# Probability copies on two engines, another order of the sample's turns, and identity products behind the norms

## The reference

```
h = rmsnorm(x);  qa,ka,va,qb,kb,vb = h @ w_in          # 8 heads a, 8 heads b (2 kv heads), 64 wide
qa,ka,qb,kb: rmsnorm per head, then rotary on the first 16 columns
oa = dilated attention (windows 128/512/2048, steps 1/4/16, merged by their softmax weights)
ob = attention over the last 128 keys, with a sink per head
x += concat(rmsnorm(oa), rmsnorm(ob)) @ w_out
x += (silu(h2 @ w_gate) * (h2 @ w_up)) @ w_down         # h2 = rmsnorm(x), 2816 hidden columns
```

## Time and profile before

| | us |
|---|---|
| median of three runs (3018.22 to 3023.43) | 3021.51 |
| profiled execution, whole | 3009.97 |
| its span, first to last instruction | 3008.4 |
| attention stage of the first layer | 294 to 600 |
| first layer's FFN | 765 to 1508 |
| second layer | 1511 to 2994 |

### The profile page before, as it was taken

The page is one execution under the profiler, slowest core; times in us unless marked ns, Lnnn a source line. Parts: engine busy times, 40 slices in busy tenths (PEclk is TensorE's granted clock), DMA queues, the critical chain, the costliest instruction groups (busy, mean ns, idle before and its releaser), DMA issues.

```text
span 3008.4 us, 51127 instructions
## 1 busy us (share of the span) xinstructions
PE 2827.9 (94%) x19000; PEld 2607.7 (87%) x19000; DVE 1171.7 (39%) x2420; ACT 916.4 (30%) x1662; POOL 510.6 (17%) x211
## 2 busy tenths in 40 slices
PE   5999999878999999999969999997889999999998
PEld 5999666578999999999969986665889999999998
DVE  5454555443322222222255455554442222322223
ACT  2343665521212111121134346664121111211110
POOL 1221000022112211122022200001222111221110
PEclk7999999978999999999979999998989999999999
DMA  5221544132654454411022144321345544454111
GB/s 162 58 64 56 151 119 111 32 98 98 197 182 158 163 174 155 155 42 55 1 94 61 54 122 128 105 78 40 100 155 166 173 155 155 155 169 155 42 42 58
DMA packets 182636, 333.47 MB, mean 111 GB/s; under 512 B 30352, under 2 KB 142096, under 8 KB 179664
## 3 DMA queue, kind: packets, MB, share of 16 engines
q1 hardware_dynamic: 171632, 195.26, 21.2%
q0 software_dynamic: 2816, 135.99, 13.6%
q10 hardware_dynamic: 8032, 0.17, 0.2%
HBM read 309.15 MB, written 157.94 MB: 155 GB/s over the span
## 4 chain that ended last, share of the span: by engine, by line
PE 89%; DVE 4%; issue 2%; ACT 2%; ACTq 1%; DMA 1%; POOL 0%; SPq 0%; DVEq 0%; POOLq 0%
PE ps L402 69%; PE ps L1422 4%; PE ps L1436 4%; PE ps L1411 3%; PE ps L1335 2%; PE ps L1485 1%; PE ps L1473 1%; DVE g_lo L957 1%; PE ps L1454 1%; DVE t_buf L942 1%; PE ps L1300 1%; DVE hf L952 1%; PE ps L1461 1%; DVE hf L942 1%; ACT pt L762 1%
## 5 line engine op out<-in xcount | busy, mean ns | idle before, releaser
L402 PE MATMUL ps<-g_hi,f_hi 128*128 128x352 f32 x2496 | 812.2, 325 | 36.0 <-DVE g_lo L957 26.9
L402 PE MATMUL ps<-g_hi,f_lo 128*128 128x352 f32 x2496 | 809.4, 324 | 0.0
L402 PE MATMUL ps<-g_lo,f_hi 128*128 128x352 f32 x2496 | 808.3, 324 | 0.0
L402 PEld LDWEIGHTS ps<-g_hi,f_hi 128*128 128x128 f32 x2496 | 473.8, 190 | 38.9 <-DVE g_lo L957 28.7
L623 POOL TENSOR_TENSOR f_lo<-f_raw,f_hi 128x2048 fp32r<-128x2048 f32 x66 | 303.9, 4618 | 1186.3 <-ACT f_hi L874 1186.3
L402 PEld LDWEIGHTS ps<-g_lo,f_hi 128*128 128x128 f32 x2496 | 474.0, 190 | 0.0
L402 PEld LDWEIGHTS ps<-g_hi,f_lo 128*128 128x128 f32 x2496 | 473.9, 190 | 0.0
L1260 DVE TENSOR_TENSOR silu<-silu,ps 128x352 f32<-128x352 f32 x132 | 68.8, 521 | 810.7 <-ACT silu L896 810.7
L1270 DVE TENSOR_TENSOR xm<-xm,ps 128x352 f32<-128x352 f32 x528 | 271.2, 521 | 199.4 <-PE ps L402 199.4
L402 PE MATMUL ps<-a_hi,f_hi 128*128 128x352 f32 x1056 | 340.6, 323 | 0.0
L402 PE MATMUL ps<-a_hi,f_lo 128*128 128x352 f32 x1056 | 338.4, 320 | 0.0
(11 more groups left out here) (167 smaller groups left out, 3473.4 us busy)
## 6 DMA issues: line engine op xcount, KB each, us to landing
out_dram<-in_cache_a_dram POOLq DMA_DIRECT2D x16, 8176.0 KB, 27.2
f_raw<-in_w_gate_up_dram SPq DMA_DIRECT2D x44, 1024.0 KB, 6.4
f_raw<-in_w_down_dram SPq DMA_DIRECT2D x22, 1024.0 KB, 4.9
k_near<-in_cache_a_dram SPq DMA_DIRECT2D x16, 1024.0 KB
v_near<-in_cache_a_dram SPq DMA_DIRECT2D x16, 1024.0 KB
w_raw<-in_w_in_dram SPq DMA_DIRECT2D x28, 512.0 KB, 4.0
k_far<-in_cache_a_dram SPq DMA_DIRECT2D x16, 768.0 KB
v_far<-in_cache_a_dram SPq DMA_DIRECT2D x16, 768.0 KB
```

The source lines that it names most:

```text
L402: mm = pe.matmul(out, left(a, c), right(b, c), start=(start and c == 0 and k == 0), stop=(stop and c == n - 1 and k == 2))
```

## The change

`keep_probs` is split: ScalarE copies the groups of hh = 0, VectorE those of hh = 1, at the end of its step, each with a semaphore of its own, and `turn_probs` and `mix` wait for the owner's. The sample's turns have another order: near 0, far 0, near 1, far 1, near 2 of the next sample (uses 3 to 7), then the first, second and third turn of the probabilities (8 to 10), far 2 (11), `mixed` (12), near 3 (13), the out products (14), far 3 (15). The sinks' exponentials come with the first turn, their sum and inverse with the third, and the spread is four slots. TensorE gets `keep_clock(n, bank)`: n fp32 products of the identity with 512 columns of a mask into a bank that nobody reads: seven ahead of the sums of norms 0 and 1, two ahead of those of norm 3, and at norms 0, 1 and 3 one ahead of the spread and three behind it.

```diff
-        pt_ready = Signal("pt_ready", len(groups))
+        groups_by = [[g for g in range(len(groups)) if groups[g][1] == hh] for hh in range(2)]
+        pt_ready = [Signal(f"pt_ready{hh}", len(groups_by[hh])) for hh in range(2)]
...
         def use_near(b, pr):
-            return 2 * pr if b == 0 else use_of(b - 1, 3 + 2 * pr)
+            return 2 * pr if b == 0 else use_of(b - 1, (3, 5, 7, 13)[pr])
+
+        def use_far(b, pr):
+            return 2 * pr + 1 if b == 0 else use_of(b - 1, (4, 6, 11, 15)[pr])
...
-        TURNS = 9 + 16 * (NB - 1) + 12 + 5 * (NP - 1)
+        TURNS = 9 + 16 * (NB - 1) + 12 + 4 * (NP - 1)
...
-                        sp.wait_ge(s_filled.sem, s_filled.at(l, max(use_near(b - 2, NP - 1) + 1, use_last(b - 2)) + 1))
+                        sp.wait_ge(s_filled.sem, s_filled.at(l, max(use_far(b - 2, NP - 1), use_last(b - 2)) + 1))
...
+                def keep_probs(d):
+                    for g in groups_of[d, 1]:
+                        _, _, a, b = groups[g]
+                        if g >= 4:
+                            dve.wait_ge(mixed.sem, mixed.at(l, groups[g - 4][0] + 1))
+                        dve.wait_ge(p_turned.sem, p_turned.at(l, g + 1))
+                        nc.vector.tensor_copy(pt[:, g % 4, 0:(b - a) * P], ps[:, 0 + g % 2, 0:(b - a) * P]
+                                              ).then_inc(pt_ready[1].sem, 1)
...
                     for _ in range(FILL[2 * (d + 2) + 1]):
                         next(beside)
+                    if 0 <= d < ND:
+                        keep_probs(d)
...
+                        if b in SPREAD_AFTER:
+                            add_sinks(SPREAD_AFTER[b])
+                        yield
+                        if b + 1 < NB:
+                            keep_far(b + 1, 2)
+                            yield
...
+            def keep_clock(n, bank):
+
+                for _ in range(n):
+                    pe.matmul(ps[:, bank, :], ident[:], mask_a[:, 0:512], start=True, stop=True)
+
             def sum_squares(l, k, acc):
 
                 first, n, before, width = NORMS[k]
+                if k in (0, 1):
+                    keep_clock(7, 7)
+                elif k == 3:
+                    keep_clock(2, 7)
                 pe.wait_ge(sq_added.sem, sq_added.at(l, ADDS[k] + n - 1))
...
             def spread_roots(l, k, bank):
 
+                if k != 2:
+                    keep_clock(1, 7)
                 pe.wait_ge(rs_ready.sem, rs_ready.at(l, 2 * k + 2))
...
                 mm.then_inc(rs_spread.sem, 1)
+                if k != 2:
+                    keep_clock(3, 0)
...
                         if g >= 2:
-                            pe.wait_ge(pt_ready.sem, pt_ready.at(l, g - 1))
+                            owner = groups[g - 2][1]
+                            pe.wait_ge(pt_ready[owner].sem, pt_ready[owner].at(l, groups_by[owner].index(g - 2) + 1))
...
-                    pe.wait_ge(pt_ready.sem, pt_ready.at(l, groups_of[d, 1][-1] + 1))
+                    for hh in range(2):
+                        pe.wait_ge(pt_ready[hh].sem, pt_ready[hh].at(l, groups_by[hh].index(groups_of[d, hh][-1]) + 1))
```

More of the change, by code:

```diff
@@ L754, in softmax @@
                                          accum_out=sum_p[:, 2 * d + hh:2 * d + hh + 1]).then_inc(exped.sem, 1)
-                def keep_probs(d, hh):
-                    for g in groups_of[d, hh]:
+                def keep_probs(d):
+                    for g in groups_of[d, 0]:
                         _, _, a, b = groups[g]
@@ L787, in exps_b, with sum_sinks @@
                                          ).then_inc(s_exped.sem, 1)
-                def spread(p):
+                def sum_sinks(p):
                     act.wait_ge(exped.sem, exped.at(l, 32 * p + 32))
@@ L805, in sample @@
                         if b + 1 < NB:
[L806 to L813, removed]
+                            keep_near(b + 1, 0)
+                            exps(b)
+                            yield
+                            exps_b()
+                            yield
+                            keep_near(b + 1, 1)
+                            yield
+                            yield
+                            keep_near(b + 1, 2)
+                            yield
                         else:
@@ L831, in sample @@
                         yield
+                        if b + 1 < NB:
+                            keep_near(b + 1, 3)
+                            yield
                         yield
+                        if b + 1 < NB:
+                            yield
                         if b in SPREAD_AFTER:
[L834 to L839, removed]
+                            for _ in range(4):
+                                yield
                 beside = sample()
@@ L852, in _ @@
                         next(beside)
-                    if 0 <= d < ND:
-                        keep_probs(d, 1)
                 next(beside, None)
-                spread(NP - 1)
+                sum_sinks(NP - 1)
                 meet(act, l, 0)
@@ L1112, in scale_b, with add_sinks @@
                                             ).then_inc(s_sums.sem, 1)
-                def spread(p):
+                def add_sinks(p):
                     dve.wait_ge(sink_exped.sem, sink_exped.at(l, 2 * p + 2))
@@ L1119, in spread @@
                     nc.vector.reciprocal(inv_p[:], sum_p[:, 32 * p:32 * p + 32]).then_inc(sums_ready.sem, 1)
-                    yield
+                def spread(p):
                     dve.wait_ge(mix_kept.sem, mix_kept.at(l, 16 * p + 16))
@@ L1458, in turn_far @@
                 def turn_far(b, pr):
-                    bank = sample_bank(use_near(b, pr) + 1)
+                    bank = sample_bank(use_far(b, pr))
                     for c in range(4):
@@ L1504, in sample @@
                         read(use_near(b, NP - 1))
-                        read(use_near(b, NP - 1) + 1)
                         score_sample(b, 0, 0, WIN)
                         yield
+                        read(use_far(b, NP - 1))
                         score_sample(b, 1, WIN, NKEYS)
@@ L1518, in sample @@
                             keys_in(b + 1)
[L1519 to L1523, removed]
+                            turn_near(b + 1, 0)
+                            yield
+                            turn_far(b + 1, 0)
+                            yield
+                            turn_near(b + 1, 1)
+                            yield
+                            turn_far(b + 1, 1)
+                            yield
+                            turn_near(b + 1, 2)
+                            yield
                         else:
```

47 lines of the change are left out of this document (31 added, 16 removed).

## The result

The changed kernel takes 2998.84 us (median of four, 2998.26 to 2999.71) against 3019.86 for the kernel before (four, 3014.71 to 3023.43) on the same chip: ratio 0.9932, 95% interval 0.9915 to 0.9949. In a later series it was 0.9940 (0.9926 to 0.9954). The forecast was 3001.5. A version in which they fill the waits ahead of the work that follows is faster than both kernels (0.9895).

The account below looks back on a forecast made before the run. TensorE ends nearly every link of the chain of waits, so only shortening or filling its queue helps. Attention 23 us gained less 3 lost at the norms makes 20: 3021.5 to 3001.5, range 2988 to 3020.

Parts of the forecast that it names:

- Wait on the copies: Attention: probability-times-value products wait 18.1 us behind ScalarE's copies; moving hh = 1 to VectorE gains 10 (4 to 18.1).
- The term of VectorE's queue: Attention: copies standing in order ahead of VectorE's masks and drains cost 2.4 us per layer (0 to 22).
- Turn of the probabilities: Attention: the sample's turn no longer stands third behind a bank ScalarE still reads; 4.1 us gained.
- New-order waits: Attention: the sample's new slot order brings waits of its own, 5.1 us lost per layer (0 to 10).
- The three-slot half-steps: Attention: four half-steps per layer hold three slots, the third needing the first's bank; 1.03 us lost each.
- Clock: Attention: half-clock stretches follow stalls that go away; 10 us gained over both layers (0 to 17).
- clock still falls: Rival, 0.18: half-speed stretches of attention stay because thin steps remain; only 10 us gained, 3011.5.
- The rival of VectorE in ScalarE's place: Rival, 0.10: VectorE's in-order copies hold up masks and bank drains, 22 us lost per layer; 3041.
- The 12 us named as the sign of a wrong forecast: Wrong if TensorE's products or scores stand behind VectorE's copies or masks for more than 12 us per layer.
- Norm 1: Three identity products behind the spread stand on the path ahead of norm 2's sums; 1.9 us lost per layer.
- the rival of the later clock: Rival, 0.05: norm 1's spread does not help the clock return, norm 2's sums end 1.9 us later; 3005.
- the products hold the clock: Rival, 0.07: identity products keep full clock at norms 0, 1 and 3, 7 us gained per layer; 2984.5.

Follow-up runs that it names:

- the later run: The changed kernel itself once more, unaltered, beside its variants on the same chip: 2999.39 us, ratio 0.9940 to the kernel before.
- the kernel without the three: Changed kernel without the three identity products behind the spread of norm 1, all others kept: 2996.01 us, ratio 0.9928 to the kernel before.
- fill at norm 1: Changed kernel with eight identity products instead of one ahead of norm 1's spread and none of three behind it: 2991.54 us, ratio 0.9914 to the kernel before.

## Why the prediction was right

The total came out, 20 gained expected and 21 measured, and so did the attention's share. Inside that share several terms were mis-sized and cancelled, so that the total came so close is in part luck.

**Attention, 23 gained expected.** By the traces the first add of norm 1 stands at 591.17 instead of 601.89; 0.6 of that came with norm 0, so 10.1 us are the stage's, and 10.2 in the second layer: 20. The run of the attention changes alone says the same, 21. Inside, term by term:

- Wait on the copies: 10 gained expected, 3.6 measured (18.1 to 14.5). The copies alone gained 8.8; the sum had no term for what the new order does to this wait, which is 5.2 of loss beside the copies. The term of VectorE's queue, 4.8, was the nearest to it. The longest of these waits in the first layer shows how: the copies stand behind the scaling of the sample's probabilities, which in the copies alone came after them (wait 0.32).
```profile
428.97 0.68 DVE L1124 TENSOR_SCALAR p_s<-p_s,st_s 128x900 f32<-128x900 f32 x1
429.56 1.28 DVE L1072 COPY pt<-ps 128x512 f32<-128x512 f32 x2
...
430.99 0.77 PE L1478 MATMUL ps<-pt,v_all 128*64 128x128 f32 x10 [1.47 <-DVE pt L1072]
```
- Turn of the probabilities: 4.1 gained expected, 3.7 lost (7.8). The step that failed counts one turn per layer that stands in the half-step of its own scaling, at about 1 us. The first layer has four such waits, 3.9 us in all (1.48, 0.57, 0.53 and 1.29); in three of them the last part of the scaling stands behind two masks, as the step says, and in one behind a drain of far keys. The mechanism was right and its count was not. The longest:
```profile
336.45 0.69 DVE L1063 CUSTOM_DVE_ANT_0 p_a<-ps,mask_a 128x512 f32<-128x512 f32 x1
...
337.07 0.69 DVE L1063 CUSTOM_DVE_ANT_0 p_a<-ps,mask_a 128x512 f32<-128x512 f32 x1
...
337.68 0.27 DVE L1129 TENSOR_SCALAR p_s<-p_s,st_s 32x132 f32<-32x132 f32 x1
338.34 0.41 PE L1580 MATMUL ps<-ident,p_s 128*128 128x128 f32 x2 [1.48 <-DVE p_s L1129]
```
- New-order waits: 10.2 lost expected; rows show 0.3 at the far turns and 1.2 at the last turn of the sample's probabilities, besides the 3.7 above. The three-slot half-steps, the greater part of this price, hardly wait.
- Spreads 8.1 and out products 5.8 expected, 8.1 (10.3 to 2.2) and 5.8 measured.

The net of these is 38.3 - 24.5 - 0.3 - 1.2 = 12.3 by the rows and was 13 in the sum.

- Clock, 10 expected: six stretches of 34.1 us in all became four of 13.7; half of the difference is 10.2, an estimate of what that is worth (the sums of a norm took 3.77 us at half clock and 2.10 at full). The granted clock of the stage is 0.99, above the 0.97 named. It differs from one execution to the next: three profiles of the old attention have 30.7 to 34.1 us at half, eight of the new one 10.2 to 23.9, so by half the differences the gain lies between 3 and 12 us. The rival "clock still falls", which had nothing gained here, is out; its reason is not, since one of the four stretches that are left (513.54) follows no wait that the timeline lists in the 8 us ahead of it.

The rival of VectorE in ScalarE's place came nearer than its 0.10 says: TensorE stands behind VectorE's copies 7.3 us per layer, and with the scaling, the far turns and the inverse sums 12.5 ((14.5 + 7.8 + 0.6 + 2.2)/2). It is faster all the same, because the greater part replaced a wait on ScalarE and the inverse sums were VectorE's before. The 12 us named as the sign of a wrong forecast asked how long TensorE waits for VectorE; it should have asked how much longer it waits in all.

**Norm 1, 1.9 lost expected:** 1.87 measured in the first layer (8.31 less 6.44) and 2.64 in the second (9.09 less 6.45); 2.7 and 1.8 in the two layers of the later run, against the kernel without the three. In the first layer the clock came back at 609.1, 2.0 us behind the first product and 4.1 behind the spread's start at 605.01:
```profile
598.87:609.11 10.24, 4.79 (x13) 2.70 (x13) 5.70 (x5) 2.77 (x4) 4.56 (x2) 0.50 0.01 2
609.11:615.93 6.82, 3.65 (x23) 2.60 (x21) 2.97 (x3) 1.88 (x4) 0.00 (x0) 1.00 0.00 0
```
The kernel before took 4.1 and 5.4 from dense work to the return, so the spread's nine transposes counted, as the sum had it, and the rival of the later clock is out: it had the return at 4.1 to 5.4 behind the first product, and in the four places of the two profiles of the changed kernel it came 1.9 to 3.7 behind it (4.0 to 5.8 behind the spread's start).

**Norm 0:** sums at 3.77 and the spread 0.96 late behind the product in the gap (0.9 expected); in return the chain gives the projections' first 144 products 24.00 us where it gave 25.14, and 26.08 in the attention alone (1.1 to 2.1 gained, 1.2 expected). **Norm 3:** sums 2.78 and 3.58 instead of 3.67, inside the 0 to 1.9 expected, and the product in the gap takes it back (the spread's 732.03 is 1.33 behind the reciprocals at 730.70, before 0.37): from the start of the sums to the first chunk it is 6.77 and 7.45 us, before 6.73 in both layers. All three together: 3 lost expected, 5.5 (3 to 8.4) measured in the kernel before; beside the new attention the ratios put it between 1 gained and 2 lost, with intervals several us wide. That is inside the ends, and no run shows it more closely.

**The base.** The sum was made on a profiled execution 11.5 us under the median and shifted by that. By the first profile the change gains 11.1, by the medians 21.0. The second profile of the kernel before lies 6.4 higher, 4.3 of it the adds of norm 1 in two layers (13.92 + 13.86 - 2 x 11.74). The other few us of the median were not found in a trace. The loss of 5.1 us at norms 1 and 2 of the first layer that a comparison of the two profiles shows is 1.9 of products, 1.7 of this, and 1.3 of the first 60 products behind norm 1 (12.59 us against 11.33). Those took 12.64 in the attention alone too, where the clock came back 6.1 us behind the first of them; in the kernel before it was 3.3.

The rival "the products hold the clock" (0.07) was wrong for this change and right as a mechanism: it put 17 us between itself and the forecast, and with the waits filled the time is 13.6 us below the changed kernel's of the same series. For this change the argument against it held: norm 0's seven products end 7.84 us ahead of the sums, and the sums run at half clock.

## What to carry to other kernels

Fill the idle time just ahead of the work that should be fast: products that ended 7.84 us ahead of the sums left them at 3.77 us, products that filled the wait had them at 2.10. And put nothing between two steps of a dependent chain, where even 1.8 us of saved sums (3.77 to 1.99) were eaten by 3.8 us of products. When a copy moves to another engine, look at what the same change puts ahead of it there: alone the copies took their wait from 18.1 to 9.3 us, beside the new order only from 21.2 to 14.5. Profile the kernel before twice, before a difference of a few us in one stage is put down to the change.

## What was not expected of the hardware

**Who starts first between VectorE and GpSimd.** Three adds of 1056 columns took 6.59 us when the first began 0.02 us ahead of GpSimd's subtraction, which then took 3.45; and 8.78 when it began 0.02 us behind, the subtraction taking 2.35. First profile of the kernel before, then the second:
```profile
607.11 6.59 DVE L942 TENSOR_TENSOR hf<-hf,sq 128x1056 f32<-128x1056 f32 x3 [1.15 <-ACT sq L671]
607.13 3.45 POOL L587 TENSOR_TENSOR f_lo<-f_raw,f_hi 128x1024 fp32r<-128x1024 f32 x1 [0.18 <-POOL f_hi L584]
```
```profile
608.05 2.35 POOL L587 TENSOR_TENSOR f_lo<-f_raw,f_hi 128x1024 fp32r<-128x1024 f32 x1 [0.18 <-POOL f_hi L584]
608.07 8.78 DVE L942 TENSOR_TENSOR hf<-hf,sq 128x1056 f32<-128x1056 f32 x3 [1.15 <-ACT sq L671]
```
The second layers agree (6.60 with the add ahead, 8.72 with it behind). What began second took longer by about one instruction of what began first: the adds 2.19 us more, beside a subtraction of 2.35; the subtraction 1.10 more, beside an add of 1.3. In six places of other runs the add begins 0.06 to 0.08 us behind the subtraction, and the three take 8.71 to 8.77. That the order of the two starts decides is read from these ten places; no run moved one of the starts on purpose.

**Transposes held the clock and brought it back** as products did, by the run that filled the waits with them: behind 7.21 us of transposes and 0.91 us of idle the spread of norm 1 took 1.23 us and the sums 2.10, where with products (second layer, fill at norm 1) they took 1.21 and 2.10; and at the start of the program the clock went from 0.50 to 1.00 under transposes alone, 4.8 us behind the first of them.
